# Order of work in a second attention stage: a value unit in two token tiles, a dense half unit and small matmuls ahead of an attention turn, and one pair's exponentials head by head

## The reference

```python
q, gl, mq = split_cols(h @ w_in, [NSA_WIDTH, 3 * NSA_HEADS, MEM_WIDTH])
gates = jax.nn.sigmoid(gl...)
k_c, v_c, k_s, v_s, k_w, v_w = (rmsnorm(x, g_kv) @ w_kv)...      # kv by six parts
k_cmp = gelu(flat(k_c) @ w_ck1) @ w_ck2      # v_cmp likewise with w_cv1, w_cv2
o_c = softmax(q k_cmp - slope * dist, masked) @ v_cmp            # blocks
o_s = softmax(q k_s   - slope * dist, masked) @ v_s              # selected
o_w = softmax(q k_w   - slope * dist, masked) @ v_w              # window
o   = gate0 * o_c + gate1 * o_s + gate2 * o_w                    # 8 heads of 64
m   = softmax(mq @ mem_k.T) @ mem_v                              # 4 heads of 128
x   = x + concat(o, m) @ w_out
```

## Time and profile before

| | |
|---|---|
| three executions | 903.67 us median (903.50, 903.67, 904.66) |
| the profiled execution, own time | 904.41 us |
| its span | 902.7 us |
| PE busy | 893.2 us, 99% of the span |
| DVE, ACT busy | 647.7 us (72%), 492.0 us (54%) |
| mean granted TensorE clock | 0.998 of full speed |

### The profile page before, as it was taken

How to read it: one execution, slowest core, us unless ns; L and a number is a source line. 1 busy time by engine, 2 the same in 40 slices (tenths; PEclk the granted TensorE clock), 3 DMA queues, 4 the chain that set the end, 5 groups by cost and what they waited for, 6 DMA issues and landing times.

```text
span 902.7 us, 18665 instructions
## 1 busy us (share of the span) xinstructions
PE 893.2 (99%) x7875; PEld 866.0 (96%) x7875; DVE 647.7 (72%) x1188; ACT 492.0 (54%) x841; POOL 44.0 (5%) x50
## 2 busy tenths in 40 slices
PE   8999999999999999999999999999999999999998
PEld 7999999999999998789999999999988999999998
DVE  6887657877767689775887767677678486565664
ACT  6663555564545566674665546447437455444451
POOL 1000001000000000000100001001132000000000
PEclk9999999999999999999999999999999999999999
DMA  9643343565454543722556554654162255555541
GB/s 348 251 175 115 136 158 137 221 238 190 159 220 183 202 158 124 277 94 94 200 188 242 207 203 164 222 199 153 38 232 94 82 208 219 194 187 202 201 158 47
DMA packets 25570, 160.68 MB, mean 178 GB/s; under 512 B 2960, under 2 KB 4880, under 8 KB 6800
## 3 DMA queue, kind: packets, MB, share of 16 engines
q1 hardware_dynamic: 24912, 158.45, 47.9%
q10 hardware_dynamic: 576, 1.05, 0.3%
HBM read 158.18 MB, written 1.05 MB: 176 GB/s over the span
## 4 chain that ended last, share of the span: by engine, by line
PE 92%; DVE 5%; DMA 1%; ACT 1%; issue 0%; SPq 0%
PE ps L395 90%; PE ps L411 1%; DVE wl L1246 1%; DMA raw<-in_w 1%; DVE arena L1677 1%; ACT arena L2308 0%; DVE col L1254 0%; DVE arena L1693 0%; DVE arena L1976 0%; SPq L2534 0%; DVE arena L1672 0%; DVE arena L1747 0%; ACT arena L2066 0%; DVE arena L1964 0%; DVE arena L1304 0%
## 5 line engine op out<-in xcount | busy, mean ns | idle before, releaser
L1246 DVE TENSOR_TENSOR wl<-raw,wh 128x1024 fp32r<-128x1024 f32 x282 | 331.5, 1224 | 124.3 <-ACT wh L2036 124.0
L395 PE MATMUL ps<-xh,wh 128*128 128x256 f32 (+1 forms) x1264 | 352.4, 279 | 2.8 <-DVE wl L1461 1.6
L395 PE MATMUL ps<-xl,wh 128*128 128x256 f32 (+1 forms) x1264 | 350.3, 277 | 0.0
L395 PE MATMUL ps<-xh,wl 128*128 128x256 f32 (+1 forms) x1264 | 350.2, 277 | 0.0
L2036 ACT CAST wh<-raw 128x1024 fp32r<-128x1024 f32 x282 | 278.9, 1047 | 120.2 <-PE ps L395 107.9
L395 PEld LDWEIGHTS ps<-xh,wh 128*128 128x128 f32 x1264 | 237.6, 188 | 5.5 <-issue 2.3
L395 PEld LDWEIGHTS ps<-xh,wl 128*128 128x128 f32 x1264 | 237.7, 188 | 0.0
L395 PEld LDWEIGHTS ps<-xl,wh 128*128 128x128 f32 x1264 | 237.7, 188 | 0.0
L395 PE MATMUL ps<-fh,wh 128*128 128x256 f32 x528 | 145.7, 276 | 0.0
L395 PE MATMUL ps<-fl,wh 128*128 128x256 f32 x528 | 145.7, 276 | 0.0
L395 PE MATMUL ps<-fh,wl 128*128 128x256 f32 x528 | 145.7, 276 | 0.0
(11 more groups left out here) (249 smaller groups left out, 1047.6 us busy)
## 6 DMA issues: line engine op xcount, KB each, us to landing
raw<-in_w SPq DMA_DIRECT2D x145, 1024.0 KB, 4.9
raw<-in_w ACTq DMA_DIRECT2D x4, 256.0 KB, 5.7
xt<-in_x SPq DMA_DIRECT2D x4, 256.0 KB, 6.7
arena<-in_mem SPq DMA_DIRECT2D x1, 1024.0 KB, 8.8
out<-xt SPq DMA_DIRECT2D x8, 128.0 KB, 1.9
arena<-in_sel SPq DMA_DIRECT2D x3, 256.0 KB, 6.1
small<-in_small SPq DMA_DIRECT2D x1, 623.0 KB, 5.8
memkv<-in_gmask SPq DMA_DIRECT2D x1, 512.0 KB, 9.4
```

Source lines behind the costliest of these rows:

```text
L395: return pe.matmul(out, lhsT, rhs, start=start, stop=stop, skip_group_check=True)
L1246: v.tensor_tensor(L[:, s], src[:, s], f32(H[:, s]), ALU.subtract).then_inc(*w_lo.up(2 * S[i] + a))
```

## The change

Nothing is computed otherwise; instructions change their order on three engines.
- PE: unit kvv is computed in two parts, the first token tile where it was, the second behind the squeezes of ck0 and ck1 and ahead of turn(0).
- PE: the second half of Bm0, and behind it kvm, come ahead of turn(2); before, turn(2), kvm and the half followed in this order.
- DVE: scores(1) ahead of probs(0); the low part of Bq1 ahead of the scaling of the values `vv`; the memory queries of Bm0 ahead of probs(3).
- ACT: the copy of the squeezed keys ahead of the exponentials of turn 2; the copies of turn(2) between the exponentials of the two heads of turn 3.

```diff
-        unit_t("kvv", lambda: 2, CH, CL, kv_in)
+        unit_t("kvv", lambda: 2, CH, CL, kv_in, turn=(0,))
         nsa_scores(1)
         squeeze(0, 0, 0)
         squeeze(0, 1)
+        unit_t("kvv", None, CH, CL, kv_in, turn=(1,))
         nsa_turn(0)
...
         last.then_inc(*ps.full("gT"))
-        nsa_turn(2)
+        part_f("Bm0", 1, range(4, 8), x_b)
         P = ps.open("kvm", 2)
...
         last.then_inc(*ps.full("kvm"))
-        part_f("Bm0", 1, range(4, 8), x_b)
+        nsa_turn(2)
         blocks_scores(0, (7, 0))
...
         rests("kvv", 2)
+        nsa_scores(1)
         nsa_probs(0)
-        nsa_scores(1)
+        rests("ck0", 2)
         d.wait_ge(*ps.ready("kvv.0"))
...
         last.then_inc(*ps.freed("kvv.0"))
-        rests("ck0", 2)
         nsa_probs(1)
...
+        by_rs("Bm0", mqB_[:, 0:512], rs_[:, 0:T], 128.0 ** -0.5)
         nsa_probs(3)
-        by_rs("Bm0", mqB_[:, 0:512], rs_[:, 0:T], 128.0 ** -0.5)
...
-        def nsa_exps(j):
-            for g in range(2):
+        def nsa_exps(j, heads=(0, 1)):
+            for g in heads:
...
         casts("cv0", 2)
+        squeezed(0)
         nsa_exps(2)
-        squeezed(0)
         squeezed(1)
         gelu()
         casts("cv1", 2)
-        nsa_exps(3)
+        nsa_exps(3, (0,))
         nsa_turned(2)
+        nsa_exps(3, (1,))
         casts("Bm0", 2)
```

## The result

| | before | after |
|---|---|---|
| median (range), 21 executions each | 903.96 us (903.46 to 905.77) | 902.85 us (902.38 to 903.48) |
| ratio, with its 95% interval | | 0.9985 [0.9979, 0.9991] |
| profiled execution, own time / span | 904.41 / 902.7 us | 903.10 / 901.4 us |

The changed kernel is faster by 0.15%, which is clear of zero and less than the 0.2% that the forecast called a change. 901.5 us was forecast: the time lies inside the range, 1.35 us above the point, where rival B had put it (902.9).

The account below looks back on a forecast made before the run. PE bounds the kernel, busy 893.2 of 902.7 us, so only its waits and low clock can be won. 904.41 - 0.79 (Part 1) - 2.26 (Part 2) = 901.4 us, given as 901.5, range 900.5 to 903.7.

Parts of the forecast that it names:

- rival B: From turn 3's second head on, ACT and DVE take the gain back; Part 2 gives 0.8 us, 902.9 us; chance 14%.
- What bounds the kernel: Whole program: only PE's 9.5 us of idle time and its work below full speed can be won.
- Part 1: At Bq1: its low part ahead of vv, scores(1) earlier, kvv in two tiles shrink PE's wait; -0.8 us.
- scores(1) ready by 355.99: DVE's start in Part 1: PE's scores(1), expected at 355.83, must be done by then, 0.16 us to spare.
- Part 2: Around turn(2): dense half of Bm0 and kvm ahead remove waits and low clock; blocks_scores 3.05 us earlier, 2.26 its own.
- the thin place at blocks_turn: Blocks_in's chain on DVE and ACT ends at 395.9 at the latest, blocks_turn comes at 396.1; 0.2 us left.
- Rival A: Clock falls at the light products from kvm to out(2), now in one piece; costs 1.15 us, 902.5 us; chance 22%.
- D: Clock falls at gT and stays low through turn(2), ACT's second head slides behind; slower, 905.7 us; chance 7%.
- The median against the profile: Of three executions of the kernel before, one had the clock's fall, costing 0.95 us; gain 3.0 against it, 2.1 against the median.

Follow-up runs that it names:

- p1_dve_vv: Kernel before with one edit: on DVE, Bq1's low part ahead of the scaling of vv; 902.88 us, ratio 0.9986.
- p2_only: Kernel before with all the change's edits except those of kvv, scores(1), probs(0), vv and Bq1's low part; 903.51 us, ratio 0.9994.
- a_no_split: Changed kernel with both heads' exponentials of turn 3 ahead of turn(2)'s copies again; 904.48 us, ratio 1.0000.
- r_before: Kernel before, unedited, timed again with the clock of every execution; 904.01 us.
- f_nosplit: Changed kernel with first memory head's maximum and exponential ahead of the blocks', and turn 3's exponentials unsplit ahead of turn(2)'s copies; 904.41 us, ratio 1.0005.
- f_dve: Changed kernel with only DVE's maximum of the first memory head ahead of blocks_in, ACT's order kept; 903.07 us, ratio 0.9985.

## Why the prediction came out as it did

- **What bounds the kernel: right.** Only PE's waits and its clock were to be had, and both are what changed.
- **Part 1, 0.79 us: right, with too much credited to it.** Bq1's wait went from 0.98 to 0.17 us, and Bq1 starts 0.84 us earlier within the stage. Its term was vv's 0.79 us on DVE, and p1_dve_vv shows that this edit alone gives as much as all of Part 1. The condition that I put on it, scores(1) ready by 355.99, was needed by the change's order only.
- **Part 2 up to out(2): right.** blocks_scores came 3.45 us earlier for 3.05, because kvm at full clock takes 0.72 us (385.34 - 384.62) where the row at the lower clock had 1.12 (gT took 0.17 us less than its term and turn(2) 0.20 more). ACT's copies of turn(2) did not hold out(2), and without the split they do, by 1.71 us for the forecast's 1.3.
- **Part 2 from out(2) on: the step that failed.** "turn(3), at 396.98 - 3.05 = 393.9, has 2.5 us left." That margin was counted from probs(3) alone. turn(3) also needs bank 4, a wait that the forecast left out, and in the changed kernel ACT empties it at 395.5. turn(3) stands 43.76 us behind kvv instead of the 42.6 of the forecast, and Part 2 was worth 0.18 us at full clock (p2_only) instead of the 1.3 that its 2.26 leaves there. The second head's exponentials, blocks_in at 391.4 (391.76 - 0.43 = 391.33 in the trace) and the thin place at blocks_turn were read rightly; with bank 4 out of the way blocks_turn waits 0.21 us, and the kernel comes to 901.58 to 901.71, which is the forecast's 901.4 within 0.3. Rival B had the size (902.9) and the engines, with the chain up to blocks_turn as the place instead of bank 4 at turn(3). That its size fits is in part luck: of its 0.8 us for Part 2, all but the 0.18 is the fall of the clock that the profile of before had caught.
- **Rival A and D: did not come.** Clock 1.0 in all 32 executions. Light products in one piece did not bring the fall as long as no wait stood among them. The Trainium skill (TensorE: Matmul & The Clock Gate, "A second HAM failure mode: psum-queue depth-cycling") tells of a kernel in which short idle times between groups of matmuls came often enough to make the clock fall again and again. a_no_split agrees in that no long idle time was needed, with 9 falls in 11; it differs in that a single wait of 1.71 us stood there. The section does not say which waits do it, and here not all do.
- **The median against the profile: right in kind, short in size.** The forecast read the three times as two without the fall and one with it, and put its cost at 0.95 us. For the fall in the trace that was about right (0.77 and 0.85 us against r_before's profile), but the 38 falls in 94 executions cost 1.4 in the middle; why most are dearer, no trace shows. Removing it is part of the result: of the 1.1 us between the medians (903.96 to 902.85), 0.3 is the share of falls that the kernel before has in its own (903.96 against 903.65 at full clock).

## What to carry to other kernels

When work moves forward on the engine that bounds, list for each of its next groups every wait that the code states, the banks it writes as well as the data it reads, and give each its own time; a wait that had slack has no bracket in the trace of before, though the rows give its size (here 0.88 us between the exponential's end and turn(3)). When two pieces use one bank, the reader of the first, wherever it stands in its own engine's list, is a condition for the second. And where a fall of the clock is in play, time many executions with their clocks: one profile caught it whole, and the median holds only a share of it.

## What the runs showed of the hardware

An idle time of TensorE of much the same length was followed by a fall of the clock in one place and not in another. Behind the block scores (32 matmuls of 15 columns) a wait of 1.7 us goes with the fall in 19 of 22 executions (a_no_split and f_nosplit). Behind a dense half of 24 matmuls of 256 columns, waits of 1.38 to 1.75 us (the changed kernel and f_dve) go with none in 42, and in p2_only with none in 11; two of these 53 show 0.999. In the kernel before, waits of 0.64 and 0.24 us behind gT's products of 30 columns go with it in 38 of 94. No run changed the work before a wait alone, so what in it makes the difference stays open.

The fall need not wait for the work behind the idle time: in a_no_split it began inside the wait, in f_nosplit 1.3 us after out(2) had started again. Three traces have it. The clock was low for 3.4 us in the kernel before and in f_nosplit (mean clock 0.998 in both) and for 6.8 us in a_no_split (0.996). In a_no_split and f_nosplit the executions at 0.998 have medians of 904.47 and 904.28 us, those at 0.996 905.26 and 905.23, against 902.57 to 902.81 without the fall. In the kernel before, the executions at 0.998 lie 0.3 to 2.4 us above the median at full clock, 1.4 in the middle; what makes one fall dearer than another there, no trace shows.
